# Level five of a blockwise triangular inverse on 32x32 array tiles

## Chip, core and metric

One core of one Trainium2 chip runs the whole program. The metric is the device time of one execution in microseconds (us), the median of several runs.

## What is computed

The kernel computes three residual layers over 512 tokens with model width 1024: an attention layer, an RWKV-7 layer (each with an MLP), and a layer with an S5 and an LRU branch. The change touches only the scan of the RWKV-7 layer, which runs in two directions over 16 heads with 64 channels:

```python
def rwkv7_scan(r, w, k, v, kk, a):
    def step(state, inp):
        r_t, w_t, k_t, v_t, kk_t, a_t = inp
        sa = jnp.einsum('bhvk,bhk->bhv', state, -kk_t)
        state = (state * w_t[:, :, None, :] + sa[..., None] * (kk_t * a_t)[:, :, None, :]
                 + v_t[..., None] * k_t[:, :, None, :])
        return state, jnp.einsum('bhvk,bhk->bhv', state, r_t)
```

## The kernel before

The program is written engine by engine with semaphores; each engine works through its own list in order. The scan is done in chunks: the 512 tokens are NCH = 8 chunks of CH = 64. Within a chunk the recurrence becomes a triangular system, whose inverse T (64x64 for each chunk, head and direction) is wanted. `over_pairs` (L396) walks over 8 pairs of heads (numbered 0 to 7 here). A tile is 128 partitions by 512 columns: head e of the pair (e = 0, 1) lies on the 64 partitions from 64e, chunk c on the 64 columns from 64c. The direction d (0, 1) has its own tiles and PSUM banks.

T is made by levels. After level l the diagonal blocks of width 2^(l+1) are right, and the step from one level to the next is a product of three matrices: T's own block, the block of L that couples the two halves, and T's other block. For each level l = 1 to 5 (LEVELS is 6, level 0 is a masked copy) and both directions:

- TensorE, L960 with helper `each` (L860, matmul at L865): A = L^T T, for each chunk and head one product with 64x64 stationary and 64x64 moving values, so 16 products. The matmuls and weight loads of this helper all carry L865. It waits for the T of the level before (`t_updated`).
- ACT, L1521 to L1523 (copy in the helper `taken`, L1497): the half of A's columns that the level needs goes to X (`x_taken`).
- TensorE, L966 with helper `each_half` (L899, matmul at L904): B = TT^T X, where TT is T transposed; 64x64 stationary and 64x32 moving values, 16 products (`dt_ready`).
- DVE, L2067 to L2073: a masked copy (L2070) takes from B only the entries of the level's off-diagonal block into T (`t_updated`), and below level five T is transposed into TT (`t_turned`).

Float32 products run as two passes, so one product is two weight loads and two matmuls in the trace, and a burst of 16 products is 32 matmul records and 32 loads.

In TensorE's list, level five stands like this: behind the second product of level four of direction 1 come 32 products of `each_stacked` (L895); then the two first products of level five (L865, directions 0 and 1); then the second product of direction 0 (L904); then `each_turned` (L870, matmul at L873) with the turned values; then the second product of direction 1 (L904). After that the chunk loop begins (L994): its first matmuls (L1004) wait for `turned` and `v_turned`; its products with T (L1022) wait for T of level five and for ACT. L1044, L1048 and L1058 are matmuls of that loop, L882 and L885 those of the scores at the start of a pair.

In ACT's list, between level four and level five: two copies for each direction out of `each_stacked` (L1533, L1534, in the trace at L1497), then, but for the last pair, `decays` for the next pair (three exponentials, L1444, L1445 and L1447), then the copies to X of level five, then two copies of the turned values (L1538, `v_turned`), then the chunk loop. In DVE's list the work for the previous pair's output (L2028 to L2042) stands between level four and level five.

Of the kernel before, what the change touches and what calls it, by code (L numbers as in the profile page):

```python
# [22 lines left out]
HEAD = 64  # L23
# [8 lines left out]
CH = 64  # L32
NCH = SEQ // CH
LEVELS = 6
# [179 lines left out]
def program(nc, t, out):  # L214

    ctx = ExitStack()
    with ctx:
        def sb(name, width):
            return ctx.enter_context(nc.sbuf_tensor(name, [P, width], F32))
# [3 lines left out]
        def sem(name):  # L223
            if name not in sems:
                sems[name] = ctx.enter_context(nc.semaphore(name))
            return sems[name]
# [8 lines left out]
        h = sb("h", DT * SEQ)  # L235
# [32 lines left out]
        def bank(b, width=SEQ):  # L268
            return ps[:, b * SEQ:b * SEQ + width]
# [17 lines left out]
        def const(name, i=0, width=P):  # L287
            return consts[:, CONSTS[name] + i * width:CONSTS[name] + (i + 1) * width]
# [15 lines left out]
        def columns_of_level(a, l, h):  # L304

            return a.rearrange("p (b h w) -> p b h w", h=2, w=1 << l)[:, :, h, :]
# [75 lines left out]
        R = [{name: over_mixes[8 + 4 * d + n] for n, name in enumerate(["Ma", "M0", "M1", "T"])} for d in range(2)]  # L382
# [196 lines left out]
        def _(pe):  # L579
# [116 lines left out]
            for half in range(2):  # L696
                mm = nc.tensor.matmul(bank(4 + half)[0:16, :], rel_sb, onehot[:, half * SEQ:(half + 1) * SEQ],
                                      start=True, stop=True)
# [47 lines left out]
            for j in range(5):  # L746
                pe.wait_ge(y_taken, t0 + j - 1)
                first = SHAPE["qk"][0] * DT + j * DT
                b = b0 + first // UPB
                pe.wait_ge(sem("weights_split"), SPLIT_COUNT[b])  # L750
                for tok in range(4):
                    for x in range(DT):
# [7 lines left out]
                        mm = nc.tensor.matmul(y, low, w_hi, start=False, stop=x == DT - 1)  # L760
# [48 lines left out]
            def hidden_product(n, step, d, b):  # L809

                k = 2 * step + d
                rows = slice(d * HEAD, (d + 1) * HEAD) if step < 2 else slice(0, P)
                nc.tensor.matmul(bank(4 * d + b), lora2[rows, k * P:(k + 1) * P],  # L813
                                 [lo_w, lo_w, lo_a, lo_a, lo_g[0], lo_g[1]][k][rows, :],
                                 start=True, stop=True).then_inc(sem("z_ready"), 1)
# [44 lines left out]
            def each(out, a, b):  # L860

                for c in range(NCH):
                    for e in range(2):
                        rows, at = slice(e * HEAD, (e + 1) * HEAD), slice(c * CH, (c + 1) * CH)
                        mm = nc.tensor.matmul(out[rows, at], a[rows, at], b[rows, at], start=True, stop=True)  # L865
                return mm

            def each_turned(out, a, by="eye"):

                for c in range(NCH):  # L870
                    for e in range(2):
                        rows, at = slice(e * HEAD, (e + 1) * HEAD), slice(c * CH, (c + 1) * CH)
                        mm = nc.tensor.matmul(out[rows, at], a[rows, at], const(by, 0, CH)[rows, :],  # L873
                                              start=True, stop=True)
                return mm
# [23 lines left out]
            def each_half(out, a, b, l, h):  # L899

                for c in range(NCH):
                    for e in range(2):
                        rows, at = slice(e * HEAD, (e + 1) * HEAD), slice(c * CH, (c + 1) * CH)
                        mm = nc.tensor.matmul(columns_of_level(out[rows, at], l, h), a[rows, at],  # L904
                                              columns_of_level(b[rows, at], l, h), start=True, stop=True)
                return mm

            A, B, C, O = [[bank(4 * d + x) for d in range(2)] for x in range(4)]

            def out_variances(n):  # L910
# [6 lines left out]
            def pair(parity, n, prev, nxt):  # L917
# [33 lines left out]
                for l in range(1, LEVELS):  # L951
                    for d in range(2):
                        k = 2 * (l - 1) + d
                        if l == 1:
                            pe.wait_ge(sem("l_copied"), n(2, d + 1))
                        if l == 1:
                            pe.wait_ge(sem("t_started"), n(2, d + 1))
                        else:
                            pe.wait_ge(sem("t_updated"), n(10, k - 1))
                        each(A[d], R[d]["L"], R[d]["T"]).then_inc(sem("x_ready"), 1)  # L960
                    for d in range(2):
                        k = 2 * (l - 1) + d
                        if l > 1:
                            pe.wait_ge(sem("t_turned"), n(8, k - 1))
                        pe.wait_ge(sem("x_taken"), n(10, k + 1))
                        each_half(B[d], R[d]["TT"], R[d]["X"], l, 1 - d).then_inc(sem("dt_ready"), 1)  # L966
                        if nxt and l <= 2 and d == 0:
                            if l == 1:
                                pe.wait_ge(sem("lora2_landed"), nxt(16, 16))
                                pe.wait_ge(sem("masked_v"), n(6, 2))  # L970
                            else:
                                pe.wait_ge(sem("z_taken"), nxt(6, 2))
                            for other in range(2):
                                hidden_product(nxt, l - 1, other, 2)
                        if l == 3:
                            if nxt:
                                pe.wait_ge(sem("z_taken"), nxt(6, 4))
                            else:
                                pe.wait_ge(sem("masked_v"), n(6, 2))
                            if prev:  # L980
                                pe.wait_ge(sem("deviation"), prev(2, d + 1))
                            each_stacked([C[d], O[d]], F[d], F[d]["ro"]).then_inc(sem("scores_ready"), 1)
                        if l == 4:
                            pe.wait_ge(sem("masked_v"), n(6, 2 * d + 4))
                            each_stacked([C[d], O[d]], F[d], const("eye", 0, CH), False
                                         ).then_inc(sem("scores_ready"), 1)
                        if l == 5 and d == 0:
                            pe.wait_ge(sem("v_staged"), n(1, 1))
                            pe.wait_ge(sem("turned"), n(4, 2))
                            each_turned(O[0], v_st, "center").then_inc(sem("scores_ready"), 1)  # L990
# [3 lines left out]
                for j in range(NCH):  # L994
                    for d in range(2):
                        k = 2 * j + d
                        c = j if d == 0 else NCH - 1 - j
# [3 lines left out]
                        for e in range(2):  # L1001
                            rows, crossed = slice(e * HEAD, (e + 1) * HEAD), slice((1 - e) * HEAD, (2 - e) * HEAD)
                            if j == 0:
                                mm = nc.tensor.matmul(A[d][crossed, 0:CH], R[d]["Ma"][rows, at], v_u[e][rows, at],  # L1004
                                                      start=True, stop=True)
                            else:
                                mm = nc.tensor.matmul(A[d][crossed, 0:CH], F[d]["al"][rows, at], s_sb_rw[j % 2][d][rows, :],
                                                      start=False, stop=True)
# [4 lines left out]
                    for d in range(2):  # L1013
                        k = 2 * j + d
                        c = j if d == 0 else NCH - 1 - j
# [4 lines left out]
                        for e in range(2):  # L1020
                            rows = slice(e * HEAD, (e + 1) * HEAD)
                            mm = nc.tensor.matmul(A[d][rows, CH:2 * CH], R[d]["T"][rows, at], w_sb[d][rows, :],  # L1022
                                                  start=True, stop=True)
                        mm.then_inc(sem("u_ready"), 1)
                    if j:
                        for d in range(2):
                            c = j if d == 0 else NCH - 1 - j
                            at = slice(c * CH, (c + 1) * CH)
                            for e in range(2):
                                rows = slice(e * HEAD, (e + 1) * HEAD)  # L1030
                                nc.tensor.matmul(O[d][rows, at], s_sb_rw[j % 2][d][rows, :], F[d]["ro"][rows, at],
                                                 start=True, stop=False)
# [3 lines left out]
                    for d in range(2):  # L1036
                        k = 2 * j + d
                        c = j if d == 0 else NCH - 1 - j
# [3 lines left out]
                        if j < NCH - 1:  # L1042
                            for e in range(2):
                                mm = nc.tensor.matmul(C[d][e * HEAD:(e + 1) * HEAD, 0:CH], F[d][("ka", "be")[e]][:, at],  # L1044
                                                      v_u[e][:, at], start=True, stop=True)
                            mm.then_inc(sem("s_ready_rw"), 1)
                        for e in range(2):
                            mm = nc.tensor.matmul(O[d][e * HEAD:(e + 1) * HEAD, at], v_u[e][:, at], R[d][("M0", "M1")[e]][:, at],  # L1048
                                                  start=j == 0, stop=True)
                        mm.then_inc(sem("o_ready_rw"), 1)  # L1050

                    if j < NCH - 1:
                        for d in range(2):
                            c = j + 1 if d == 0 else NCH - 2 - j
                            at = slice(c * CH, (c + 1) * CH)
                            for e in range(2):
                                rows, crossed = slice(e * HEAD, (e + 1) * HEAD), slice((1 - e) * HEAD, (2 - e) * HEAD)
                                nc.tensor.matmul(A[d][crossed, 0:CH], R[d]["Ma"][rows, at], v_u[e][rows, at],  # L1058
                                                 start=True, stop=False)
# [55 lines left out]
            for n in range(2 * LT):  # L1115
                pe.wait_ge(y_taken, t0 + n - 1)
                if n % UPB == 0:
                    b = b0 + n // UPB
# [1336 lines left out]
```

## Time and profile before

| what | value |
|---|---|
| median of 3 runs | 2386.7 us (2384.76 to 2389.63) |
| time of the profiled execution | 2394.83 us |
| its span, first to last instruction | 2392.7 us |
| mean granted clock of TensorE | 0.977 of full |
| TensorE busy (PE) | 2250.3 us |
| weight loads (PEld, beside PE) | 1712.6 us |
| DVE, ACT, POOL busy | 1246.5, 943.4, 735.8 us |
| scan stage (8 pairs) | about 905 to 1360 us |
| L904, L865 in that stage | 90.9, 87.5 us |

Times in the views are microseconds from the start of the span. PE is TensorE's matmuls, PEld its weight loads, ACT is ScalarE, DVE VectorE, POOL GpSimd. The end of a matmul is modelled, and successive matmuls overlap, so the start of the next group says more than the duration of one. "issue" is time in which an engine waited for nothing that the profile shows.

### The profile page before, as it was taken

To read this page: it belongs to the slowest core of one execution; us is meant where nothing else is said; L and a number is where in the kernel's file an instruction comes from. 1 tells how busy PE (TensorE), PEld (TensorE's weight loads), DVE (VectorE), ACT (ScalarE), POOL (GpSimd) and SP (SyncE) were. 2 spreads that over 40 slices of the span, in tenths; PEclk is the share of its full clock that TensorE was granted. 3 is DMA by queue.
4 is the path that set the end of the run, shared out by engine and by line. 5 is a ranking of instruction groups with operands and counts; after the bars stand their busy time and mean duration, and the time that the engine had idled before them with its cause. 6 is when DMAs were issued, how large, how long until landed. Compare 5 with 4: busy or idle time off the path is not lost.

```text
span 2392.7 us, 46390 instructions
## 1 busy us (share of the span) xinstructions
PE 2250.3 (94%) x19640; PEld 1712.6 (72%) x19640; DVE 1246.5 (52%) x2035; ACT 943.4 (39%) x1681; POOL 735.8 (31%) x384
## 2 busy tenths in 40 slices
PE   8999989999979998988888889999998999999998
PEld 6885778888867647777777777777887666754476
DVE  5028254023155666767777534794213999736123
ACT  4238444233234433444444443554323222343133
POOL 2310334444414203111111033444431433430246
PEclk9999999999979998999999999999997999999999
DMA  4312123233212210000000122343231333222232
GB/s 143 111 60 78 62 72 96 88 101 93 88 42 80 88 44 9 10 10 10 10 10 10 39 71 79 117 179 124 82 106 71 106 117 114 89 87 78 71 94 82
DMA packets 49882, 180.64 MB, mean 75 GB/s; under 512 B 5600, under 2 KB 5856, under 8 KB 49440
## 3 DMA queue, kind: packets, MB, share of 16 engines
q1 hardware_dynamic: 46064, 166.82, 21.6%
q10 hardware_dynamic: 3632, 11.08, 1.2%
q8 instruction: 148, 2.42, 0.4%
q14 instruction: 38, 0.31, 0.0%
HBM read 167.33 MB, written 10.55 MB: 74 GB/s over the span
## 4 chain that ended last, share of the span: by engine, by line
PE 72%; issue 12%; DVE 5%; ACT 5%; POOL 4%; DMA 0%; POOLq 0%; ACTq 0%; DVEq 0%; SPq 0%
PE ps L603 15%; PE ps L604 15%; PE ps L605 15%; PE ps L606 6%; POOL ring_lo L2266 4%; PE ps L904 2%; PE ps L865 2%; PE ps L651 2%; PE ps L895 1%; PE ps L1101 1%; PE ps L722 1%; PE ps L737 1%; PE ps L712 1%; PE ps L1122 1%; PE ps L813 1%
## 5 line engine op out<-in xcount | busy, mean ns | idle before, releaser
L2266 POOL TENSOR_TENSOR ring_lo<-ring,ring_hi 128x1024 fp32r<-128x1024 f32 x240 | 589.8, 2465 | 1019.1 <-ACT ring_hi L1158 1019.0
L605 PE MATMUL ps<-u_lo,ring_hi 128*128 128x512 f32 x968 | 384.8, 398 | 0.0
L1158 ACT ACTIVATE ring_hi<-ring 128x1024 fp32r<-128x1024 f32 x240 | 251.4, 1052 | 105.4 <-DMA ring<-in_wall 102.0
L603 PE MATMUL ps<-mlp_u_hi,ring_hi 128*128 128x512 f32 x512 | 204.6, 400 | 13.6 <-DVE u_lo L1744 9.0
L606 PE MATMUL ps<-arena,ring 128*128 128x512 f32 x480 | 210.5, 594 | 6.0 <-ACT arena L1627 3.3
L605 PEld LDWEIGHTS ps<-u_lo,ring_hi 128*128 128x128 f32 x968 | 183.9, 190 | 43.5
L603 PE MATMUL ps<-mid_hi,ring_hi 128*128 128x512 f32 x512 | 203.3, 397 | 2.6 <-POOL ring_lo L2266 2.6
L604 PE MATMUL ps<-mlp_u_hi,ring_lo 128*128 128x512 f32 x512 | 203.2, 397 | 0.0
L605 PE MATMUL ps<-mid_lo,ring_hi 128*128 128x512 f32 x512 | 202.5, 396 | 0.0
L604 PE MATMUL ps<-mid_hi,ring_lo 128*128 128x512 f32 x512 | 202.5, 395 | 0.0
L603 PE MATMUL ps<-in_u_hi,ring_hi 128*128 128x512 f32 x480 | 193.8, 404 | 5.8 <-POOL gs_lo L2354 2.8
L604 PE MATMUL ps<-in_u_hi,ring_lo 128*128 128x512 f32 x480 | 190.7, 397 | 0.0
L606 PEld LDWEIGHTS ps<-arena,ring 128*128 128x128 f32 x480 | 90.2, 190 | 123.4 <-issue 109.6
L1909 DVE TENSOR_TENSOR arena<-ps,arena 128x512 f32<-128x512 f32 (+1 forms) x64 | 44.0, 691 | 235.5 <-ACT arena L1311 235.4
L603 PEld LDWEIGHTS ps<-mlp_u_hi,ring_hi 128*128 128x128 f32 x512 | 97.1, 190 | 39.1 <-DVE u_lo L1744 9.3
L603 PEld LDWEIGHTS ps<-in_u_hi,ring_hi 128*128 128x128 f32 x480 | 90.8, 189 | 42.7 <-issue 13.0
L603 PEld LDWEIGHTS ps<-mid_hi,ring_hi 128*128 128x128 f32 x512 | 96.2, 188 | 27.7 <-POOL ring_lo L2266 4.8
L604 PEld LDWEIGHTS ps<-mlp_u_hi,ring_lo 128*128 128x128 f32 x512 | 97.3, 190 | 22.8
L605 PEld LDWEIGHTS ps<-mid_lo,ring_hi 128*128 128x128 f32 x512 | 96.2, 188 | 23.2
L604 PEld LDWEIGHTS ps<-mid_hi,ring_lo 128*128 128x128 f32 x512 | 96.2, 188 | 23.0
L604 PEld LDWEIGHTS ps<-in_u_hi,ring_lo 128*128 128x128 f32 x480 | 91.1, 190 | 20.9 <-issue 0.2
L904 PE MATMUL ps<-ring 64*64 64x32 f32 x2560 | 90.9, 220 | 15.8 <-ACT ring L1497 12.9
(434 smaller groups left out, 4335.6 us busy)
## 6 DMA issues: line engine op xcount, KB each, us to landing
ring<-in_wall SPq DMA_DIRECT2D x273, 512.0 KB, 3.7
s_tables<-arena ACTq DMA_DIRECT2D x16, 512.0 KB, 2.7
arena<-s_tables SPq DMA_DIRECT2D x16, 512.0 KB, 3.7
arena<-bias_lines SPq DMA_DIRECT2D x16, 448.0 KB, 4.3
arena<-in_lora SPq DMA_DIRECT2D x8, 384.0 KB, 3.0
h<-in_x SPq DMA_DIRECT2D x1, 2048.0 KB, 8.0
out<-arena ACTq DMA_DIRECT2D x8, 256.0 KB, 2.9
consts<-in_consts SPq DMA_DIRECT2D x1, 1152.0 KB, 14.1
```

The lines of the kernel that those rows point to most:

```text
L603: nc.tensor.matmul(y, w_hi, high, start=x == 0, stop=False)
L604: nc.tensor.matmul(y, w_lo, high, start=False, stop=False)
L605: return nc.tensor.matmul(y, w_hi, low, start=False, stop=x == k - 1)
L606: return nc.tensor.matmul(y, ring[:, at:at + P], rhs(x), start=x == 0, stop=x == k - 1)
L651: mm = nc.tensor.matmul(bank(7)[:, b:b + 1], squares[:, b * P:(b + 1) * P], const("mean", 0, 1), start=first and b == 0, stop=last and b = ...
L712: nc.tensor.matmul(bank(score_bank(n), key_width(n)), qT[rows, at:at + P], kT[rows, keys + first * P:keys + end * P], start=True, stop=Tru ...
L722: tr = nc.tensor.transpose(bank(4 + n % 2)[:, x * P:(x + 1) * P], p_sb[n % 4][:, SINK_AT + x * P:SINK_AT + (x + 1) * P], const("ident"))
L865: mm = nc.tensor.matmul(out[rows, at], a[rows, at], b[rows, at], start=True, stop=True)
L904: mm = nc.tensor.matmul(columns_of_level(out[rows, at], l, h), a[rows, at], columns_of_level(b[rows, at], l, h), start=True, stop=True)
L1158: nc.scalar.activation(ring_hi[:, slot], ring[:, slot], ACT.Copy).then_inc(sem("weights_high"), 1)
L1909: TT(mid[:, at], out_bank(f"up{n}{part}", j), relu[j % 2], ALU.mult).then_inc(y_taken, 1)
L2266: G.tensor_tensor(ring_lo[:, slot], ring[:, slot], ring_hi[:, slot].bitcast(F32), ALU.subtract).then_inc(sem("weights_split"), 1)
```

## The change

At levels 1 to 4 nothing changes. At level five both products use a new helper `each_block`, whose 16 products contract over one contiguous half (32 rows) of a head's 64 partitions, with 32 columns of stationary and 32 columns of moving values. A product so takes a 32x32 tile of the array in place of a 64x64 one. The other halves of the PSUM tiles keep what stood there; the second product does not read them and the mask of L2070 leaves them out. The order of the bursts, the waits, the signals and the work of ACT, DVE and POOL stay as they are.

```diff
+            def each_block(out, a, b, h, rows_half):
+
+                for c in range(NCH):
+                    for e in range(2):
+                        kept, near = [slice(c * CH + x * CH // 2, c * CH + (x + 1) * CH // 2) for x in (h, 1 - h)]
+                        rows, made = [slice(e * HEAD + x * CH // 2, e * HEAD + (x + 1) * CH // 2) for x in (rows_half, 1 - h)]
+                        mm = nc.tensor.matmul(out[made, kept], a[rows, near], b[rows, kept], start=True, stop=True)
+                return mm
...
-                        each(A[d], R[d]["L"], R[d]["T"]).then_inc(sem("x_ready"), 1)
+                        if l < LEVELS - 1:
+                            each(A[d], R[d]["L"], R[d]["T"]).then_inc(sem("x_ready"), 1)
+                        else:
+                            each_block(A[d], R[d]["L"], R[d]["T"], 1 - d, 1 - d).then_inc(sem("x_ready"), 1)
...
-                        each_half(B[d], R[d]["TT"], R[d]["X"], l, 1 - d).then_inc(sem("dt_ready"), 1)
+                        if l < LEVELS - 1:
+                            each_half(B[d], R[d]["TT"], R[d]["X"], l, 1 - d).then_inc(sem("dt_ready"), 1)
+                        else:
+                            each_block(B[d], R[d]["TT"], R[d]["X"], 1 - d, d).then_inc(sem("dt_ready"), 1)
```

## Rows read from the trace of the kernel before

**Rows 1.** The page, first part: busy time, share of the span, instructions.
```profile
PE 2250.3 (94%) x19640; PEld 1712.6 (72%) x19640; DVE 1246.5 (52%) x2035; ACT 943.4 (39%) x1681; POOL 735.8 (31%) x384
```

**Rows 2.** Groups by line, 905 to 1360 us: busy us, mean ns, idle time before.
```profile
L904 PE MATMUL ps<-ring 64*64 64x32 f32 x2560 | 90.9, 220 | 15.8 <-ACT ring L1497 12.9 <-issue 2.8
L865 PE MATMUL ps<-arena,ring 64*64 64x64 f32 x2560 | 87.5, 222 | 12.0 <-DVE arena L2060 6.1 <-issue 5.9
```

**Rows 3.** Chain that ended last, level five of pair 1: start, us, what.
```profile
997.33 0.28 ACT ring L1497
...
999.87 0.59 ACT sq L1538
```

**Rows 4.** Timeline of PE, level five of pair 1: start, us, group.
```profile
997.75 1.12 PE L904 MATMUL ps<-ring 64*64 64x32 f32 x32 [0.32 <-ACT ring L1497]
998.67 1.16 PE L873 MATMUL ps<-consts,arena 64*64 64x64 f32 x32
999.63 1.10 PE L904 MATMUL ps<-ring 64*64 64x32 f32 x32
```

**Rows 5.** Views of single lines, weight loads: ns min/median/max; array tile, 128, 64, 32 columns.
```profile
L932 PEld LDWEIGHTS ps<-arena x112: 186/188/189, 955.6 to 1318.0; 128*128 128x128 f32 x112
...
L904 PEld LDWEIGHTS ps<-ring x2560: 129/135/223, 911.1 to 1350.4; 64*64 64x64 f32 x197
...
L1101 PEld LDWEIGHTS ps<-arena,s5c x128: 106/110/110, 1887.1 to 2045.9; 128*32 128x32 f32 x128
```

**Rows 6.** Timeline of PE, scores of pair 1, on four tiles in turn.
```profile
966.09 0.22 PE L882 MATMUL ps<-ring_hi_values 64*64 64x64 f32 x1
966.10 0.22 PE L885 MATMUL ps<-ring_hi_values 64*64 64x64 f32 x1
966.10 0.22 PE L882 MATMUL ps<-ring_hi_values 64*64 64x64 f32 x1
966.11 0.22 PE L885 MATMUL ps<-ring_hi_values 64*64 64x64 f32 x1
966.15 0.22 PE L882 MATMUL ps<-ring_hi_values 64*64 64x64 f32 x1
```

**Rows 7.** Timeline of PE, chunk loop of pair 1.
```profile
1003.26 0.29 PE L1044 MATMUL ps<-sq,arena 128*64 128x64 f32 x4
1003.37 0.29 PE L1048 MATMUL ps<-arena,sq 128*64 128x64 f32 x4
1003.59 0.45 PE L1058 MATMUL ps<-sq,arena 64*64 64x64 f32 x8
```

**Rows 8.** Stretches, busy us (records) PE, PEld, DVE, ACT, POOL, clock; queue q8, 988.90 to 995.94.
```profile
929.30:933.30 4.00, 3.36 (x130) 3.25 (x129) 2.58 (x5) 0.77 (x2) 0.00 (x0) 1.00 0.02 4
...
988.90:992.38 3.48, 3.18 (x127) 3.04 (x128) 2.58 (x5) 0.77 (x2) 0.00 (x0) 1.00 0.02 5
...
q8 instruction: 2, 0.03, 1.9%
```

**Rows 9.** Chain that ended last, level five of pair 5.
```profile
1231.70 1.57 issue
1233.27 2.08 PE ps L865 x64
...
1236.26 0.99 PE ps L873 x32
```

**Rows 10.** Stretches as in rows 8, and PE's timeline ahead of level one, level five (pair 0).
```profile
909.00:920.43 11.43, 11.43 (x202) 9.86 (x202) 6.41 (x9) 3.73 (x6) 0.00 (x0) 0.56 0.01 1
970.48:977.56 7.08, 7.08 (x204) 6.27 (x204) 5.07 (x8) 3.73 (x6) 0.00 (x0) 1.00 0.02 5
...
937.70:941.10 3.40, 2.06 (x83) 1.95 (x74) 0.00 (x0) 3.07 (x7) 3.40 (x3) 1.00 0.03 5
...
908.96 2.49 PE L865 MATMUL ps<-arena,ring 64*64 64x64 f32 x64 [2.13 <-DVE arena L2060]
...
941.09 1.12 PE L904 MATMUL ps<-ring 64*64 64x32 f32 x32 [1.34 <-ACT ring L1497]
```

## The prediction

> **What bounds the kernel now.** I read the page first: TensorE is busy for 94% of the span [rows 1]. The change touches two lines of the scan stage only, so I took the groups of that stage next (905 to 1360 us): the two products of the levels, L904 and L865, are its costliest groups, 90.9 and 87.5 us over five levels and eight pairs of heads [rows 2]. Level five is a fifth of each. Busy time says nothing of order, so the third view is the chain of work that ended last, around level five of the second pair [rows 3], and the fourth the timeline of TensorE there [rows 4]. What is to be seen: while TensorE works on the two first products of level five (L865), ACT still owes level four two large copies and then three exponentials for the next pair, and only at 997.33 does it come to the copy of X for direction 0. TensorE waits for that copy, starts the second product of direction 0 at 997.75 (L904), goes on to the turned values (L873) at 998.67, and ACT's two copies after L873 release the chunk loop. The second product of direction 1 (999.63) runs beside those copies. So of the four bursts that the change shortens, one lies on the path: L904 of direction 0. The two of L865 end before ACT is ready or at about that time (in pairs 5 and 7 the chain does run through them [rows 9], see the supply below), and the last is covered by the copies L1538.
>
> **The bursts.** Each is 32 matmul records and 32 weight loads (16 products in float32, two passes each). A burst of 64x64 operands and one of 64x32 take the same time from start to start of the next: L904, half as wide in what moves, hands over after 0.92 and L873 after 0.96 us [rows 4]. So the moving columns, which the first product now halves too, are worth nothing; 0.94 us for 16 rounds is 59 ns per round, two array tiles working side by side. What sets the round? The weight load: its record is 188 ns for 128 columns, 135 for 64 and 110 for 32 [rows 5], that is 53 and 25 ns less, or 0.8 ns a column; 64 columns are some 53 ns of the 59. With 32 columns that part halves and the round becomes 59 - 26 = 33 ns, the burst 0.53 us: 0.42 us less. The first matmul's latency stays. The bound on the good side is 0.42; on the bad side nothing is gained, if something per instruction sets the round. The scores speak against the latter [rows 6]: with four tiles in use four matmuls start in the 0.06 us from 966.09 to 966.15, with their loads, which is 15 ns a matmul, and 33 ns a round of two is no faster than that. I take 0.42.
>
> The Trainium skill ("TensorE: Matmul & The Clock Gate", "Wait — 56ns, not 53.3ns?") states that successive matmuls never start less than about 25 ns apart, however small they are. By it, as an estimate, a burst would take 32 x 25 = 0.8 us and gain 0.14 instead of 0.42, and the whole sum would come to -0.3 us, 2386.4. The 15 ns above [rows 6] disagree with that floor, at least for matmuls on different tiles.
>
> **Switching tiles.** L873 still uses 64x64 tiles, so TensorE now changes the tile size between L904 of direction 0 and L873, and back before direction 1; two more changes lie before level five and before the chunk loop, where it waits anyway. The nearest rows are a change from 128x64 to 64x64: L1058 starts 0.22 us after L1048, where L1048, of the same four records but without a change of tile, had started 0.11 us after L1044 [rows 7]. So a change costs about 0.1 us. From below it is nothing, from above perhaps 0.2, if a smaller tile drains worse. One lies on the path in each pair: the gain on the path is 0.42 - 0.1 = 0.3 us.
>
> **The instruction supply.** The chain names stretches of "issue" in the dense parts of the scan, such as 1.57 us at 1231.70 [rows 9]. They are not random: between the ends of two such stalls there are 130+129 and 127+128 records of matmuls and loads [rows 8], that is 256 instructions with a few strays, and in the stretch of two such blocks (988.90 to 995.94) the instruction queue moves two packets, 0.03 MB. A block takes 3.48 to 4.0 us from stall end to stall end even when TensorE could do it faster. In pair 5 a stall ends at 1231.70 + 1.57 = 1233.27 [rows 9]; the block behind it holds the four bursts of 64 instructions up to the end of L873, which ends at 1236.26 + 0.99 = 1237.25 in the records, with its last start some 0.2 earlier. The next block can't come before 1233.27 + 3.5 = 1236.8 and may come as late as 1237.2: in this pair TensorE would be faster and then wait, and between 0 and 0.25 us is left. The last pair has the same pattern. I take 0.1 for each of these two. In the other six the block boundary lies elsewhere (in the first products, in L904 after a long idle time, or behind L873) and the 0.3 stands.
>
> **The rest of the path.** What follows starts when ACT is done with L1538, and that is released by L873: it moves with it. The update of T in direction 1 on DVE has to be ready one product later; it is released by a burst that itself ends earlier. DVE's backlog from level four doesn't bound the loop, since TensorE's waits there name ACT. The instruction count is the same, no wait and no DMA is added, and SP, POOL and HBM see nothing. The stale halves of PSUM that ACT still copies cost what they cost before.
>
> Sum: 6 x 0.3 + 2 x 0.1 = 2.0 us. The profiled execution took 2394.8 us with a span of 2392.7, so it would become 2392.8; it lies 8.1 us above the median of 2386.7, on which the forecast stands: 2386.7 - 2.0 = **2384.7 us**. The shown runs of before lie 4.9 us apart, more than the gain.
>
> **Rivals.**
> - The clock (slower). With the first products done in 1.1 instead of 2.0 us, the idle time ahead of L904 grows in the pairs where ACT is late: in pair 0 from 1.34 to about 2.2 us [rows 10]. Ahead of 908.96 there was an idle time of 2.13, and in the 11.43 us behind it the clock was 0.56 of full, that is mostly at the lower of its two levels, 1.2 GHz. The price: the same work took 7.08 us at full clock in the next pair, 4.35 us less; at half for 0.88 x 11.43 = 10 us, that is 0.43 us for each us at half. Three pairs (0, 2, 4) have such an idle time. One fall of 3.4 us each costs 3 x 1.5 = 4.4: with the gain +2.4, 2389.1. If each lasts as long as the first (10 us), 3 x 4.35 - 2.0 = +11, 2397.7. It decides for "slower" from (4.8 + 2.0) / 0.43 = 16 us at half clock. Against it: idle times of 1.3 us in a stretch as empty (2.06 us of work in 3.4 from 937.7) left the clock full.
> - The change doesn't do what it says: something fixed per instruction of one tile sets the round and it stays at 59 ns. Only the change of tile is left, 8 x 0.1, 2387.5; with a round half way between 33 and 59 ns, 8 x (0.21 - 0.1) = 0.9 gained, 2385.8. The equal times of L865 and L904 are for it, and that no burst here loads fewer than 64 columns at this pace; the loads are against it [rows 5]. The Trainium skill's floor, named above, belongs to this case.
> - All four bursts count, as if the path ran through TensorE alone and the supply of instructions were free: 32 x 0.42 less 32 changes of 0.1, -10.2, 2376.5. The idle time of 1.34 us ahead of L904 speaks against it, and so do the blocks.
>
> **Chances.** Forecast 0.53; the clock 0.17, in most of it beyond the short falls; tiles no or little faster 0.22; all bursts 0.08. A measurement of this kernel can tell some 0.2%, 4.8 us, from no change. Faster than 2381.9: the last rival and a little of the forecast's own spread, 0.13. Slower than 2391.5: 0.15 from the clock. Same: 0.72. The range takes in the forecast with the spread of the runs (2.4 each way), both cases without a gain and the short falls of the clock: 2381.0 to 2391.0.
>
> **What would show it.** Right: L904's level-five records with 32x32 tiles start at 16 rounds of about 33 ns; load records fall to about 110 ns; from the start of L904 of direction 0 to that of L873 0.6 instead of 0.92 us, and from there to the loop unchanged; the copy of X still at the end of ACT's work, with TensorE idle for 2.2 us ahead of it in pairs 0, 2 and 4; in pairs 5 and 7 an issue stall within L873. Wrong: half-clock stretches after level five (the clock), rounds near 59 ns, a change of tile of more than 0.2 us, or L865 named in the chain at level five where it wasn't.

## The result: slower by 0.7%, and TensorE's clock at half in every pair but the last

| | before | after |
|---|---|---|
| median | 2389.63 us (7 runs, 2384.76 to 2397.01) | 2407.28 us (7 runs, 2402.49 to 2415.39) |
| ratio to before | | 1.0068, 95% interval 1.0050 to 1.0086 |
| profiled execution, span | 2394.83, 2392.7 us | 2407.28, 2405.1 us |
| mean granted clock in it | 0.977 | 0.964 |

The forecast was 2384.7 us and its range ended at 2391.0. The page of the kernel after: the share of busy time is the same 94% as before, the number of instructions too. What differs is the row of the clock, in which the 17th, 19th and 21st slice, in the scan, hold an 8 where before had a 9. First the row of before, then lines of the page after:

```profile
PEclk9999999999979998999999999999997999999999
```

```profile
PE 2259.3 (94%) x19640; PEld 1718.9 (71%) x19640; DVE 1245.1 (52%) x2035; ACT 945.9 (39%) x1681; POOL 737.2 (31%) x384
...
PEclk9999999999979998898989999999997999999999
...
PE 72%; issue 12%; ACT 5%; DVE 5%; POOL 4%; DMA 0%; POOLq 0%; ACTq 0%; DVEq 0%; SPq 0%
```

A row of forty digits is coarse. Stretches cut to where the clock fell show it (length, busy us and records of PE, PEld, DVE, ACT, POOL, then the clock). There are seven such stretches at level five, one at or behind it in each pair from 0 to 6 (one more of 3.4 us stands at the end of the scan, as it did before); three of the seven:

```profile
932.50:946.20 13.70, 13.11 (x201) 11.34 (x201) 4.21 (x15) 3.13 (x12) 7.92 (x9) 0.51 0.01 2
...
994.00:1007.60 13.60, 13.01 (x201) 11.24 (x200) 7.91 (x18) 3.03 (x12) 11.20 (x10) 0.51 0.01 2
1058.80:1065.70 6.90, 6.32 (x101) 5.41 (x99) 2.56 (x7) 2.08 (x7) 6.90 (x7) 0.52 0.02 5
```

Together the seven are 75 us long, four of some 13.7 and three of 6.8. They are at the lower level, 1.2 GHz. TensorE's timeline of pair 0 shows what it did before: the first products (L914, the line of the new helper's matmul) are done in 1.1 us, then it idles for 2.07 us, and the second product already runs slowly. Before, a stretch of 3.4 us there had 2.06 us of work and an idle time of 1.34 us [rows 10].

```profile
929.26 1.11 PE L914 MATMUL ps<-arena,ring 32*32 32x32 f32 x64
932.44 1.06 PE L914 MATMUL ps<-ring 32*32 32x32 f32 x32 [2.07 <-ACT ring L1512]
933.43 1.97 PE L873 MATMUL ps<-consts,arena 64*64 64x64 f32 x32
935.33 1.06 PE L914 MATMUL ps<-ring 32*32 32x32 f32 x32
936.79 0.48 PE L1019 MATMUL ps<-sq,arena 64*64 64x64 f32 x4 [0.40 <-ACT sq L1553]
```

In pair 1 the idle time comes in two pieces, 0.83 us of waiting for instructions within the first products and 1.03 us for ACT:

```profile
992.08 0.78 PE L914 MATMUL ps<-arena,ring 32*32 32x32 f32 x42 [0.83 <-issue]
993.89 1.06 PE L914 MATMUL ps<-ring 32*32 32x32 f32 x32 [1.03 <-ACT ring L1512]
```

Added up, TensorE idles from its first products (the wait ahead of them in pair 5 counted in) to the second one for 1.9 to 2.1 us in each of the pairs 0 to 6, and for 0.51 us in pair 7, the only one without a fall. Before it was 1.0 to 1.6 us in pairs 0 to 6 and nothing in pair 7. So idle time alone could explain this trace; the experiments below decide.

L873, which nobody changed, takes 1.90 us from its start to that of the next group where it took 0.96 [rows 4]. The chain that ended last goes the same way as before (pair 1: ACT's copy of X, second product, L873, ACT's copies), only its pieces are longer; lines behind the new helper count 15 more than before.

```profile
993.47 0.28 ACT ring L1512
...
993.89 1.06 PE ps L914 x32
994.96 1.93 PE ps L873 x32
...
996.90 0.59 ACT sq L1553
```

The stages of the scan, read from the first starts of L882, L865, L873 and the loop's first matmul (L1004, after: L1019) in the two timelines, say where the 12.4 us between the two spans are. From L873 to the end of the pair, pairs 0 to 6 take 21.3 us more, for 72 us more at half clock: 0.3 us for each. From a pair's first L865 (level one) to L873 pairs 1 to 7 take 0.7 us less; within that, from the first product of level five to L873, they take 2.6 us less. Pair 0 takes 7.0 us less up to L873, because in this execution the clock did not fall there as it did before [rows 10]; that is not the change's doing.

### The profile page after: what moved, and what is told of

The parts are those of the page before. It is cut to its first block, busy times and chain, and to the rows that moved or that the text cites. A ratio compares the mean times of both kernels' runs of the same rounds, so it can differ in the third digit from the quotient of the medians.

```text
span 2405.1 us, 46390 instructions
## 1 busy us (share of the span) xinstructions
PE 2259.3 (94%) x19640; PEld 1718.9 (71%) x19640; DVE 1245.1 (52%) x2035; ACT 945.9 (39%) x1681; POOL 737.2 (31%) x384
## 4 chain that ended last, share of the span: by engine, by line
PE 72%; issue 12%; ACT 5%; DVE 5%; POOL 4%; DMA 0%; POOLq 0%; ACTq 0%; DVEq 0%; SPq 0%
PE ps L603 15%; PE ps L604 15%; PE ps L605 15%; PE ps L606 6%; POOL ring_lo L2281 4%; PE ps L651 2%; PE ps L904 2%; PE ps L865 2%; PE ps L895 1%; PE ps L1116 1%; PE ps L933 1%; PE ps L722 1%; PE ps L737 1%; PE ps L712 1%; PE ps L1059 1%
## 5 line engine op out<-in xcount | busy, mean ns | idle before, releaser
L603 PE MATMUL ps<-mlp_u_hi,ring_hi 128*128 128x512 f32 x512 | 205.1, 401 | 13.1 <-DVE u_lo L1759 8.9
L1963 DVE TENSOR_TENSOR arena<-arena,ps 128x512 f32<-128x512 f32 x16 | 11.0, 688 | 147.0 <-PE ps L605 147.0
```

The source lines that it names most:

```text
L603: nc.tensor.matmul(y, w_hi, high, start=x == 0, stop=False)
```

## The experiments

Two theories on the fall of the clock, and one that leaves it out, stand in the expectations. Idle theory: it is the longer idle time ahead of the second product. Width theory: it is how little of the array the bursts of level five use, whatever the time they take. Tile theory: small tiles, or the change of tile, slow what follows. All time at half clock below is worked out from the mean granted clock of a run as 2 x (1 - clock) x span, over the whole program, and the median over the runs is given. The kernel before has 105 to 110 us of it, most outside the scan. Its median was 2385.62 us (15 runs) beside the first four experiments, 2390.57 (31) beside the next four and 2387.97 (26) beside the last four; the three groups ran on three chips, so the ratios are to be read rather than the medians.

| kernel | median us | ratio to before, 95% | clock | us at half |
|---|---|---|---|---|
| changed kernel | 2407.28 | 1.0068 (1.0050 to 1.0086) | 0.964 | 173 |
| first products only | 2401.73 | 1.0080 (1.0049 to 1.0111) | 0.969 | 149 |
| second products only | 2389.47 | 1.0025 (1.0006 to 1.0044) | 0.978 | 107 |
| first products twice | 2425.26 | 1.0157 (1.0125 to 1.0188) | 0.961 | 192 |
| before, first products move half | 2397.72 | 1.0041 (1.0018 to 1.0063) | 0.971 | 139 |
| before, turned values early | 2382.65 | 0.9969 (0.9952 to 0.9985) | 0.978 | 105 |
| changed, turned values early | 2389.00 | 1.0005 (0.9984 to 1.0025) | 0.971 | 139 |
| changed, full-size filler | 2393.15 | 1.0016 (0.9992 to 1.0040) | 0.975 | 122 |
| changed, 64 rows | 2390.22 | 0.9999 (0.9980 to 1.0017) | 0.975 | 119 |
| 64 rows, turned early | 2388.25 | 1.0004 (0.9984 to 1.0025) | 0.974 | 124 |
| second 64 rows, turned early | 2383.68 | 0.9986 (0.9973 to 1.0000) | 0.978 | 105 |
| the same with filler | 2382.84 | 0.9974 (0.9958 to 0.9989) | 0.980 | 98 |
| before with filler | 2391.55 | 1.0029 (1.0012 to 1.0047) | 0.977 | 110 |

**One of the two products.** In the first run the second products are those of before, in the second the first ones.

```diff
-                            each_block(B[d], R[d]["TT"], R[d]["X"], 1 - d, d).then_inc(sem("dt_ready"), 1)
+                            each_half(B[d], R[d]["TT"], R[d]["X"], l, 1 - d).then_inc(sem("dt_ready"), 1)
```

> Only the first products of level five use the 32x32 tiles; the second ones stay as before. Idle theory (the clock falls because TensorE does its first products in about 1.0 us instead of 2.0 and then idles 2.1 instead of 1.3 us ahead of the second product): all of the loss is here, 10 to 18 us over the kernel before, with stretches at half clock behind level five in most of the seven pairs in which ACT is late. Tile theory (small tiles or the change of tile slow what follows, wherever they stand): about half of the loss, 5 to 9 us. Width theory (the clock falls because too few columns and rows of the array work in the stretch, wherever that is saved): most of the loss, but fewer or shorter falls than with both.

```diff
-                            each_block(A[d], R[d]["L"], R[d]["T"], 1 - d, 1 - d).then_inc(sem("x_ready"), 1)
+                            each(A[d], R[d]["L"], R[d]["T"]).then_inc(sem("x_ready"), 1)
```

> Only the second products of level five use the 32x32 tiles; the first ones stay as before. Idle theory: the idle time ahead of the second product stays at 1.3 us, so the clock stays at full level and the 0.3 us per pair that the path saves are left: 0 to 4 us under the kernel before. Tile theory: half of the loss, 5 to 9 us slower. Width theory: 3 to 12 us slower, with falls of the clock behind level five in some pairs.

The first products alone bring the loss (ratio 1.0080, 149 us at half). In this profile the clock stayed full in pair 4, with an idle time of 2.06 us, and fell for 10.2 us in pair 7, with 0.51 us; so the idle time ahead of the second product does not sort the pairs here. The second products alone lose 0.25%, with the clock's median where it was. Tile theory, which wanted half the loss from each, is weakened. In the profile of the second run the burst on the path is short as forecast and the clock full (0.62 us from L914 to L873, idle time 1.34 as before), and from L914 to the loop's first matmul pair 0 takes 3.15 us where before took 3.46 in pairs 0 and 1. But the runs show no gain: the ratio is 1.0025, two of its ten had a clock of 0.971 and took 2400 us, and the others did not fall below before's lowest. What takes the 0.3 us per pair back is not shown.

```profile
929.28 1.97 PE L865 MATMUL ps<-arena,ring 64*64 64x64 f32 x62
932.60 0.69 PE L914 MATMUL ps<-ring 32*32 32x32 f32 x32 [1.34 <-ACT ring L1512]
933.22 1.15 PE L873 MATMUL ps<-consts,arena 64*64 64x64 f32 x32
```

**The first products twice.** This was meant to fill the idle time again, with small tiles.

```diff
+                            each_block(A[d], R[d]["L"], R[d]["T"], 1 - d, 1 - d)
                             each_block(A[d], R[d]["L"], R[d]["T"], 1 - d, 1 - d).then_inc(sem("x_ready"), 1)
```

> The changed kernel, but every first product of level five is issued twice into the same place (same values), so that TensorE works as long as before ahead of the second product, on 32x32 tiles; 512 products more in all. Idle theory: the idle time is back at about 1.3 us and the clock stays full: 0 to 4 us under the kernel before. Width theory: the small tiles still count for little and the clock falls as in the changed kernel, 10 to 20 us over the kernel before. Tile theory: as the changed kernel too. In pairs 1, 3, 5 and 7, where the instruction blocks bind, the added instructions may cost up to 1 us each.

2425.26 us and 192 us at half, further above before than any theory had it. TensorE had more work and the clock fell for longer. But the idle time was not filled: in each of the eight pairs 1.1 to 1.8 us of waiting for instructions stand inside the doubled burst, 11.8 us in all; the expectation had allowed up to 1 us, and in four pairs alone. That is about the idle time of before, at which before's clock had stayed up in all but one pair, so the run speaks against idle theory without settling it, and why the clock fell for longer than in the changed kernel is not shown. The rise of 18 us above the changed kernel so has two causes, 19 us more at half (some 7 us at 0.35 to 0.4 each) and the added waits (about the rest); an estimate, since the parts weren't run apart. Pair 0:

```profile
932.38 1.54 PE L914 MATMUL ps<-arena,ring 32*32 32x32 f32 x91
935.65 1.02 PE L914 MATMUL ps<-arena,ring 32*32 32x32 f32 x31 [1.73 <-issue]
...
937.43 1.97 PE L873 MATMUL ps<-consts,arena 64*64 64x64 f32 x32
```

**Half the moving columns on full-size tiles.** The kernel before, with only the 32 columns that the level needs moved through the first products.

```diff
-                        each(A[d], R[d]["L"], R[d]["T"]).then_inc(sem("x_ready"), 1)
+                        if l < LEVELS - 1:
+                            each(A[d], R[d]["L"], R[d]["T"]).then_inc(sem("x_ready"), 1)
+                        else:
+                            each_half(A[d], R[d]["L"], R[d]["T"], l, 1 - d).then_inc(sem("x_ready"), 1)
```

> The kernel before, but the first products of level five move only the 32 columns of each chunk that the level needs; tiles stay 64x64 and the pace of 59 ns a round stays, so TensorE works for as long as before. Idle theory and tile theory: no difference, within 0.2% of before. Width theory (less work in the array, whatever the time): some falls of the clock behind level five, 3 to 10 us slower.

The edit takes nothing away but work in the array: same instructions, same tiles, same pace. It is 0.4% slower, with 139 us at half, and in the profile (of the slowest of its six runs) the clock fell at or behind level five in five pairs, two of them:

```profile
1001.20:1004.60 3.40, 3.40 (x71) 3.36 (x67) 1.97 (x5) 1.18 (x2) 2.13 (x2) 0.55 0.03 5
1233.30:1243.50 10.20, 10.01 (x156) 9.27 (x154) 5.19 (x13) 2.83 (x9) 7.94 (x8) 0.52 0.01 2
```

The idle times of level five stay near those of before, 0 to 1.4 us where before had 0 to 1.6 (the largest difference upward is in pair 1, 1.23 in place of 0.97). In pair 5, the second of the two shown, the wait ahead of the first products is 1.29 us where before had 1.57 [rows 9] and kept the clock; the bursts then follow without a gap:

```profile
1231.29 2.31 PE L904 MATMUL ps<-arena,ring 64*64 64x32 f32 x64 [1.29 <-issue]
1233.40 1.91 PE L904 MATMUL ps<-ring 64*64 64x32 f32 x32
1235.11 1.96 PE L873 MATMUL ps<-consts,arena 64*64 64x64 f32 x32
```

Neither idle theory nor tile theory allows this; it is the cleanest of the runs. It also says that halving what moves is no free saving where the loads set the pace.

**The turned values early.** L873 moves ahead of the second products, into TensorE's idle time, once in the kernel before and once in the changed one.

```diff
+                    if l == 5:
+                        pe.wait_ge(sem("v_staged"), n(1, 1))
+                        pe.wait_ge(sem("turned"), n(4, 2))
+                        each_turned(O[0], v_st, "center").then_inc(sem("scores_ready"), 1)
                     for d in range(2):
                         k = 2 * (l - 1) + d
                         if l > 1:
                             pe.wait_ge(sem("t_turned"), n(8, k - 1))
...
-                        if l == 5 and d == 0:
-                            pe.wait_ge(sem("v_staged"), n(1, 1))
-                            pe.wait_ge(sem("turned"), n(4, 2))
-                            each_turned(O[0], v_st, "center").then_inc(sem("scores_ready"), 1)
```

> The kernel before with the turned values (16 products, 64x64) issued between the first and the second products of level five, into the idle time in which TensorE waits for ACT. Path theory (the chain at level five runs ACT's copy of X, second product of direction 0, turned values, ACT's two copies): the loop no longer waits for that product and its copies start right behind the copies of X, some 1.0 to 1.5 us less per pair, 8 to 12 us in all, as far as the clock stays as it was. Clock theory (array work moved out of the stretch behind the second product lets the clock fall there): the gain is given back in part, 0 to 8 us under before, with the time at half clock in the record up by 10 us or more.

> The same move in the changed kernel, so that TensorE's idle time ahead of the second product shrinks from 2.1 to about 1.1 us, while the work in the array over the whole level stays that of the changed kernel. Idle theory (already weak): the clock stays up and the time falls to 2370 to 2378. Width theory (the little work on small tiles counts): time at half clock stays above 140 us in the record, and only the path's 8 to 12 us are won on the changed kernel, 2393 to 2400.

On the kernel before it wins 0.31%, 7.4 us by the ratio, with the clock as it was. So the reading of the chain was right: L873 was on the path. The gain is a little under the 8 to 12 us expected; something else is late next, as far as the chain of one pair shows. The chain in pair 1 of this version leaves ACT and runs through DVE: the output work of the previous pair (L2028 to L2042, then L2008) stands in DVE's list ahead of the last update of T (L2070), and L1022 waits for that.

```profile
995.43 0.72 DVE arena L2028 x2
996.15 0.45 issue
996.60 1.42 DVE arena L2032 x2
...
998.04 1.43 DVE arena L2039 x2
...
999.49 0.69 DVE arena L2042
1000.18 0.46 DVE u L2008
1000.64 0.46 DVE ring_hi_values L2008
1001.10 0.36 DVE arena L2070
...
1001.50 0.59 PE ps L1022 x5
```

In the changed kernel the move leaves 139 us at half, just under the 140 that width theory gave as the least, and wins more than forecast (2389.00 against 2393 to 2400); idle theory's 2370 to 2378 isn't reached. But the time at half does fall, from 173 us, though the work over the level is the same: where in the level the work and the gaps lie counts too.

**A full-size filler.** One product of 128x128 on 512 columns of constants in the idle time.

```diff
+                    if l == 5:
+                        for _ in range(1):
+                            nc.tensor.matmul(B[0], const("head_sum"), consts[:, CONSTS["iota"]:CONSTS["iota"] + SEQ], start=True, stop=True)
                     for d in range(2):
                         k = 2 * (l - 1) + d
```

> The changed kernel plus one product of 128x128 on 512 columns of constants (4 instructions, 0.86 us) for each pair, issued while TensorE waits for ACT ahead of the second product of level five; its result is overwritten or masked out. Width theory: a third of a microsecond or so of full-size work per pair is what the small tiles took away, so the falls of the clock go back to what before had or below: 100 to 115 us at half clock in the record and 2378 to 2390. Tile theory (small tiles slow what follows): nothing comes back, 2405 to 2412, since the filler only adds work.

Two records per pair bring the time at half from 173 to 122 us and the ratio from 1.0068 to 1.0016, a little short of the forecast of 100 to 115 us at half and 2390 us at most. Tile theory falls: the small tiles are all still there and in most pairs what follows runs at full pace. Not in all: in the profile the clock still fell for 17.1 us in pair 4 and for 3.4 us at a time behind pairs 1 and 6. The filler also shortens the idle time, so it doesn't tell the other two theories apart. In pair 0 (L975 is the filler) the second product and L873 take 0.62 and 1.08 us to the next start, in place of 0.99 and 1.90.

```profile
929.32 0.83 PE L914 MATMUL ps<-arena,ring 32*32 32x32 f32 x48
930.08 1.12 PE L975 MATMUL ps<-consts 128*128 128x512 f32 x2
932.22 0.69 PE L914 MATMUL ps<-ring 32*32 32x32 f32 x32 [1.01 <-ACT ring L1515]
932.84 1.15 PE L873 MATMUL ps<-consts,arena 64*64 64x64 f32 x32
933.92 0.69 PE L914 MATMUL ps<-ring 32*32 32x32 f32 x32
```

**64 rows.** The changed kernel, contracting over all 64 rows again (the added rows hold zeros in one factor), with 32 loaded and 32 moving columns.

```diff
-                        rows, made = [slice(e * HEAD + x * CH // 2, e * HEAD + (x + 1) * CH // 2) for x in (rows_half, 1 - h)]
+                        rows, made = slice(e * HEAD, (e + 1) * HEAD), slice(e * HEAD + (1 - h) * CH // 2, e * HEAD + (2 - h) * CH // 2)
```

> The changed kernel with products that contract over all 64 rows of a head but still load 32 and move 32 columns (64x32 array tiles): the pace is that of the changed kernel, 29 ns a round, the rows in use are doubled. If only columns count for the clock and the loads' pace, nothing changes against the changed kernel, 2402 to 2412. If the area in use counts, fewer falls, 2393 to 2402. Tile theory in its form of 32-row tiles being the fault: back to 2384 to 2390.

The loads and matmuls last as long as in the changed kernel (the view of the line in this version, loads then matmuls, first and second products):

```profile
L914 PEld LDWEIGHTS ps<-arena,ring x512: 102/110/111, 929.3 to 1338.6; 64*32 64x32 f32 x171
L914 PE MATMUL ps<-arena,ring x512: 186/193/214, 929.3 to 1338.7; 64*32 64x32 f32 x171
```

and yet the time is back at that of before, 0.9999, with 119 us at half in place of 173. The idle times are those of the changed kernel to 0.02 us, 2.07 in pair 2:

```profile
1047.45 0.96 PE L914 MATMUL ps<-ring 64*32 64x32 f32 x32 [2.07 <-ACT ring L1512]
```

The falls at or behind level five are still there in six pairs, but for 3.4 to 6.8 us each, 24 us in this profile where the changed kernel had 75. That is what speaks most plainly against idle theory. The only thing that differs is 64 rows in place of 32 at the same pace, and that brings the time back. The 2390.22 us lie at the edge of what the expectation gave for 32-row tiles being at fault, and below what it gave for the area in use. Whether it is the area or something of 32-row tiles this run alone can't say; the run with half the moving columns has no such tiles and also falls, which speaks for the former.

**Combinations.** The parts that gave something, together: the early turned values with 64 rows in both products, then in the second product only (the first as before), then with the filler; and the filler alone in the kernel before. The edits are those shown.

> Both edits that gave something so far: products of level five over 64 rows with 32 loaded columns (64x32 tiles), and the turned values issued into the idle time ahead of the second product. Sum of the terms: path of the small loads about -3 us at equal clock, path of the turned values -4 to -7, time at half clock about 120 us as in the version with 64 rows: 8 to 10 us under the kernel before. If the early turned values take away the array work behind the second product, some 140 us at half clock, and no more than 3 us are left.

> As the run before, but the first products are those of the kernel before (64x64 tiles, 64 columns moving), which mostly lie beside ACT's work anyway; only the second products use 64x32 tiles. If the work of the first products holds the clock and costs nothing on the path: time at half clock 100 to 110 us as in the kernel before, and 8 to 12 us under it. If the first products are on the path now: as the run before, or slower by up to 3 us.

> The same plus one full-size product of constants per pair (4 instructions, 0.86 us) ahead of the second products. If more work in the array keeps the clock up further: time at half clock 95 to 105 us and 1 to 3 us under the run before, as far as the product fits the idle time (1 us or less since the turned values stand there too); else it delays the second products by up to 0.8 us in 8 pairs, up to 6 us over the run before.

> The kernel before plus the full-size product in the idle time ahead of the second product of level five (1.3 us in pairs 0, 2 and 4, less in the others). If the clock of the kernel before, too, hangs on the work at level five: time at half clock 5 to 15 us under before, 0 to 5 us faster. If before's falls (110 us in the record, most of it outside the scan) have other causes: no difference in the clock, and 0 to 4 us slower for the delay in pairs 1, 3, 5 and 7.

The gains don't add up. With 64 rows in both products the early move leaves 124 us at half, as the first of its two expectations had it, and no gain (1.0004), which neither had: at that time at half 8 to 10 us were expected. What took them is not shown. With the first products of before the clock is that of before (105 us) and 0.14% is left, less than half of what was expected; the short second burst brought nothing measurable on top of the early move. The filler takes the time at half to 98 us, the lowest of all, and the ratio to 0.9974; in the kernel before it changes nothing in the clock (110 us at half) and costs 0.3%; it needs 1.06 us to the start of the next burst, more than the 0.59 us or less that TensorE idles ahead of the second product in pairs 1, 3, 5, 6 and 7 before. The versions that beat both kernels are so the kernel before with the turned values early (0.9969) and the one with early turned values, 64-row second products and filler (0.9974); their intervals overlap.

## Why the prediction was wrong, step by step

- **The burst** was sized right. 0.53 + 0.1 us was forecast from L904 of direction 0 to L873; at full clock it is 1058.10 - 1057.41 = 0.69 in pair 2 and 0.62 to 0.66 in the other pairs that were at full clock, against 0.92 before [rows 4]. The two first products together take 64 records in about 0.93 us, 29 ns a round where 33 was worked out. The loads' median is 108 ns; 110 was forecast.

```profile
1057.41 0.76 PE L914 MATMUL ps<-ring 32*32 32x32 f32 x32 [2.08 <-ACT ring L1512]
1058.10 1.56 PE L873 MATMUL ps<-consts,arena 64*64 64x64 f32 x32
...
L914 PEld LDWEIGHTS ps<-arena,ring x512: 101/108/108, 929.3 to 1359.4; 32*32 32x32 f32 x171
```

- **The floor** between matmuls that the Trainium skill gives ("TensorE: Matmul & The Clock Gate", "Wait — 56ns, not 53.3ns?"), some 25 ns, stood beside the sum. It does not hold here: 64 records in 0.93 us on two tiles are a matmul start every 15 ns.
- **The change of tile** at about 0.1 us holds: 0.62 less 16 rounds of 29 ns leaves 0.15.
- **The path** was read right: the first products weren't on it, the idle time ahead of L904 grew to 2.07 us as forecast (2.2), and moving L873 off it gained 7.4 us in the kernel before.
- **The blocks of instructions**: in pair 7 the stall within L873 came, 0.20 us. In pair 5 none came there; the clock had gone to half at its start, at 1239.5.

```profile
1360.74 1.03 PE L873 MATMUL ps<-consts,arena 64*64 64x64 f32 x28
1361.97 0.33 PE L873 MATMUL ps<-consts,arena 64*64 64x64 f32 x4 [0.20 <-issue]
```

- **The step that failed** is the weight given to the clock. The rival named the mechanism and the price (0.43 us per us at half; a line through time and time at half gives 0.40, 0.31 and 0.32 over the 15, 31 and 26 runs of before and 0.35 over the 7 of the changed kernel, and the stages above 0.3), but it counted the pairs by an idle time in one piece ahead of the second product: 3, with 3.4 or 10 us each, and gave it a chance of 0.17. It was 7 of 8, with 6.8 or 13.7 us, 75 us in all where its worse case had 30. The waits for instructions within or just ahead of the first products, about half of the idle time in pairs 1, 3, 5 and 6, were left out of the count. Its counter-argument, that an idle time of 1.3 us had left the clock full, compared the idle time alone and not what the array did in the rest of the stretch: rows x columns x moved columns of a first product fall to an eighth by the change, of a second one to a quarter. And it was written as if the clock had a margin, while before already fell once without the change [rows 10]. The small gain on the path shows in the bursts, but not in a time. An estimate: 63 to 68 us at half clock less, at 0.3 to 0.4 each, would take the changed kernel from 2407.3 to between 2380 and 2388, that is 1 to 10 us under before's 2389.6. The forecast of 2.0 lies in that range, but the range is too wide to confirm it, and the run with the second products alone, at the clock of before, was 0.25% slower and not faster.

What stays open: what exactly of the work in the array the clock follows, rows, columns or both. The runs show that fewer moving columns at the same pace (139 us) and fewer rows at the same pace (173 against 119) both cost. The run that moves L873 (139 against 173) shows that the order of the work plays a part as well. The run with the first products twice (192) has more work, on small tiles, and longer falls; it remains unexplained.

## What to carry to other kernels

In a stage that waits for another engine while TensorE's clock is full, a saving of array work that is off the path gains nothing and can have a price: here 0.3 us per pair on the path were bought with 7 to 14 us at half clock behind it. Before shrinking matmuls, look at the granted clock around the stage and for falls that are already there, and keep the full-size form of those products that lie beside another engine's work. If the chain shows idle time of the engine, first put something from the path into it: here that was the only single edit that beat the kernel before (0.9969).

## What the runs showed of the hardware

- Loading 32 in place of 64 columns takes a round of two tiles from 59 to 29 ns, whether 32 or 64 rows are used (108 and 110 ns for a load); moving 32 in place of 64 columns doesn't change the pace (0.92 and 0.96 us a burst [rows 4]).
- Once the clock had fallen, it stayed at half for some 13.7 us in four pairs, although TensorE was busy for 13.0 to 13.1 of them.
- One product on the whole array per pair (128x512, 1.06 us to the start of the next burst) is enough to take away about 50 of 68 us at half that the small tiles had added.
